# Two pages a step: sample attention over the paged cache in 16 steps

## The reference

```python
ckv_past = cache_ckv[page_table].reshape(b, past, KV_RANK)      # 8 x 2048 x 256
kr_past = cache_krope[page_table].reshape(b, past, QK_ROPE)     # 8 x 2048 x 64
keys_c = jnp.concatenate([ckv_past, ckv], axis=1)
keys_r = jnp.concatenate([kr_past, k_rope], axis=1)
sc = (einsum('bqhr,bkr->bhqk', q_lat, keys_c) + einsum('bqhe,bke->bhqk', q_rope, keys_r)) * SCALE
p = softmax(sc)
o_lat = einsum('bhqk,bkr->bqhr', p, keys_c)
```

## Time and profile before

| | |
|---|---|
| median of 3 runs | 669.1 us (668.73 to 670.76) |
| span of the profiled execution | 667.8 us, granted clock 0.927 |
| PE busy | 560.4 us, 84% |
| DVE, ACT, POOL busy | 359.6, 263.1, 162.3 us |
| DMA | 95.75 MB, mean 143 GB/s |

### The profile page before, as it was taken

The page is one execution under the profiler, slowest core; times in us unless marked ns, Lnnn a source line. Parts: engine busy times, 40 slices in busy tenths (PEclk is TensorE's granted clock), DMA queues, the critical chain, the costliest instruction groups (busy, mean ns, idle before and its releaser), DMA issues.

```text
span 667.8 us, 12482 instructions
## 1 busy us (share of the span) xinstructions
PE 560.4 (84%) x4724; PEld 469.1 (70%) x4724; DVE 359.6 (54%) x774; ACT 263.1 (39%) x571; POOL 162.3 (24%) x240
## 2 busy tenths in 40 slices
PE   2899998999999999999966146699885879999990
PEld 2799998999888888888743134345553548999980
DVE  4643987725666666444366266427775672323227
ACT  6413221123555554525143244337665552222210
POOL 4202000000000000000035274307998850112114
PEclk9989998969999999999997578799999799999996
DMA  7042122365888888887244632401232252332203
GB/s 294 32 158 95 49 90 71 113 227 164 261 270 267 267 265 272 276 272 238 87 117 100 186 100 75 182 1 44 83 101 89 95 219 99 97 92 82 80 1 128
DMA packets 46926, 95.75 MB, mean 143 GB/s; under 512 B 6489, under 2 KB 18114, under 8 KB 46354
## 3 DMA queue, kind: packets, MB, share of 16 engines
q1 hardware_dynamic: 46866, 94.94, 44.3%
HBM read 87.29 MB, written 7.73 MB: 142 GB/s over the span
## 4 chain that ended last, share of the span: by engine, by line
PE 60%; DVE 10%; POOL 8%; DMA 7%; issue 5%; ACT 4%; SPq 4%; DVEq 0%; POOLq 0%; ACTq 0%; PEldq 0%
PE pm L1163 16%; PE pm L1164 14%; PE pm L1165 14%; DMA dec<-ac_dram 4%; PE px L1225 4%; POOL xb L1137 3%; POOL hring L1142 3%; PE px L1241 3%; SPq L372 2%; PE pm L1400 2%; DVE xw_lo L787 1%; DVE r_pre L715 1%; POOL dec L1106 1%; PE pm L1447 1%; DMA w_raw<-in_w_out 1%
## 5 line engine op out<-in xcount | busy, mean ns | idle before, releaser
L1163 PE MATMUL pm<-xw_hi,w_lo 128*128 128x260 f32 x544 | 166.1, 305 | 15.9 <-DVE w_lo L685 11.4
L1164 PE MATMUL pm<-xw_lo,w_hi 128*128 128x260 f32 x544 | 157.1, 289 | 0.0
L1165 PE MATMUL pm<-xw_hi,w_hi 128*128 128x260 f32 x544 | 156.8, 288 | 0.0
L1163 PEld LDWEIGHTS pm<-xw_hi,w_lo 128*128 128x128 f32 x544 | 105.6, 194 | 33.0 <-issue 11.9
L425 ACT ACTIVATE w_hi<-w_raw 128x1024 fp32r<-128x1024 f32 (+1 forms) x56 | 57.8, 1032 | 154.5 <-PE pm L1165 153.9
L685 DVE TENSOR_TENSOR w_lo<-w_raw,w_hi 128x1024 fp32r<-128x1024 f32 (+1 forms) x56 | 67.9, 1214 | 80.6 <-ACT w_hi L425 80.5
L1164 PEld LDWEIGHTS pm<-xw_lo,w_hi 128*128 128x128 f32 x544 | 105.9, 195 | 0.2
L1165 PEld LDWEIGHTS pm<-xw_hi,w_hi 128*128 128x128 f32 x544 | 105.9, 195 | 0.0
L1163 PE MATMUL pm<-mix_hi,w_lo 128*128 128x260 f32 x256 | 72.4, 283 | 1.3 <-DVE mix_lo L986 1.3
L1164 PE MATMUL pm<-mix_lo,w_hi 128*128 128x260 f32 x256 | 72.5, 283 | 0.0
L1165 PE MATMUL pm<-mix_hi,w_hi 128*128 128x260 f32 x256 | 72.4, 283 | 0.0
(11 more groups left out here) (240 smaller groups left out, 1088.1 us busy)
## 6 DMA issues: line engine op xcount, KB each, us to landing
page<-in_cache SPq DMA_DIRECT2D x128, 288.0 KB, 3.4
w_raw<-in_w_in SPq DMA_DIRECT2D x34, 512.0 KB, 5.0
w_raw<-in_w_out SPq DMA_DIRECT2D x16, 512.0 KB, 3.6
dec<-ac_dram SPq DMA_DIRECT2D x16, 256.0 KB, 10.2
hring<-in_ssm_state SPq DMA_DIRECT2D x8, 512.0 KB, 3.5
o_ssms<-hring SPq DMA_DIRECT2D x8, 512.0 KB, 2.6
w_raw<-in_w_qb SPq DMA_DIRECT2D x6, 384.0 KB, 3.0
xraw<-in_xT SPq DMA_DIRECT2D x4, 520.0 KB, 6.0
```

Source lines behind the costliest of these rows:

```text
L1163: pe.matmul(out, wl, xh, start=start, stop=False)
L1164: pe.matmul(out, wh, xl, start=False, stop=False)
L1165: return pe.matmul(out, wh, xh, start=False, stop=stop)
```

## The change

A step is now two pages of four sequences: 16 steps, every 20 slots. Each has three places of its own: scores (`SLOT`), transposes (`TSLOT`, 10 slots on) and values (`VSLOT`, 16 slots on); all lie inside items 19 to 38. Keys and values are separate arrays in DRAM and separate buffers (`kpage`, `vpage`), each two steps deep, of the same total size. SyncE issues one DMA per sequence, page and kind: 8 of 160 KB for the keys of a step, 8 of 128 KB for its values. Steps 0 and 1 are loaded in rounds 15 and 16 of its loop; later, keys n+2 are loaded in the round after the item of scores n, and values n+2 in the round after the item of values n. The matmuls of the scores take the columns of both pages at once; values of the two pages are summed in PSUM. Probabilities and their transpose have one buffer in place of two.

```diff
-NSTEP = 2 * NPAGE
-SLOT = [divmod(16 * 19 + 3 + 32 * n // 3, 16) for n in range(NSTEP)]
-VSLOT = [divmod(min(16 * 19 + 32 * (n + 1) // 3 + 10, 16 * NIN - 1), 16) for n in range(NSTEP - 1)]
+PPS = 2
+SPG = NPAGE // PPS
+NSTEP = 2 * SPG
+SLOT = [divmod(16 * 19 + 3 + 20 * n, 16) for n in range(NSTEP)]
+TSLOT = [divmod(16 * 19 + 3 + 20 * n + 10, 16) for n in range(NSTEP)]
+VSLOT = [divmod(16 * 19 + 3 + 20 * n + 16, 16) for n in range(NSTEP)]
...
-    page = at("page", [P, 4, 4, 576], F, G_)
+    kpage = at("kpage", [P, 2, 4, PPS, 320], F, G_)
+    vpage = at("vpage", [P, 2, 4, PPS, 256], F, G_ + 20480)
...
-        def load_pages(n):
-
-            g, p, s = n // NPAGE, n % NPAGE, n % 4
-            if n >= 4:
-                sp.wait_ge(p_pn, n - 3)
+        def load_pages(what, n):
+
+            g, p0 = n // SPG, PPS * (n % SPG)
+            to, of, done, free = ((kpage, "cache_k", s_kl, p_sc), (vpage, "cache_v", s_vl, p_pn))[what]
+            if n >= 2:
+                sp.wait_ge(free, n - 1)
             for j in range(4):
-                at_ = (4 * g + j) * NPAGE + p
-                index = sp.value_load(ptab[0:1, at_:at_ + 1])
-                sp.dma_start(page[:, s, j, :], a["cache"][bass.ds(index, 1)].rearrange("a p n -> p (a n)")).then_inc(s_pl[s], 16)
+                for p in range(PPS):
+                    at_ = (4 * g + j) * NPAGE + p0 + p
+                    index = sp.value_load(ptab[0:1, at_:at_ + 1])
+                    sp.dma_start(to[:, n % 2, j, p, :], a[of][bass.ds(index, 1)].rearrange("a p n -> p (a n)")).then_inc(done[n % 2], 16)
...
-            for n in steps(i + 1):
-                load_pages(n)
+            if i in (15, 16, 17):
+                for what in range(2):
+                    if i < 17:
+                        load_pages(what, i - 15)
+            for n in steps(i - 1):
+                if n + 2 < NSTEP:
+                    load_pages(0, n + 2)
+            for n in sums(i - 1):
+                if n + 2 < NSTEP:
+                    load_pages(1, n + 2)
...
-            for n in steps(i):
-                if n:
-                    copy_ptb(n - 1)
-                sample_exp(n)
+            for place, do, n in sorted([(SLOT[n], 0, n) for n in range(NSTEP)] + [(TSLOT[n], 1, n) for n in range(NSTEP)]):
+                if place[0] == i:
+                    (sample_exp, copy_ptb)[do](n)
...
                     if 8 * r + k in place:
-                        n_ = place[8 * r + k]
-                        if n_:
-                            prob_t(n_ - 1)
-                        score(n_)
+                        score(place[8 * r + k])
+                    if (i, 8 * r + k) in TSLOT:
+                        prob_t(TSLOT.index((i, 8 * r + k)))
...
-            pe.wait_ge(s_pl[s], 64 * (n // 4 + 1))
+            pe.wait_ge(s_kl[n % 2], 64 * PPS * (n // 2 + 1))
+            out = px[:, n % 2, 0:PPS * P].rearrange("p (a k) -> p a k", a=PPS)
             for op in range(4):
                 for j in range(4):
...
-                    x = page[:, s, j, (256, 384, 512, 512)[op]:(384, 512, 576, 576)[op]]
-                    lo_, n_ = (0, 0, 0, 64)[op], (128, 128, 64, 64)[op]
-                    last = pe.matmul(px[32 * j:32 * j + 32, n % 2, lo_:lo_ + n_], w, x, start=op == 0, stop=op == 3)
+                    x = kpage[:, n % 2, j, :, (0, 128, 256, 256)[op]:(128, 256, 320, 320)[op]]
+                    half = slice((0, 0, 0, 64)[op], (128, 128, 64, 128)[op])
+                    last = pe.matmul(out[js, :, half], w, x, start=op == 0, stop=op == 3)
...
         def values(n):
             pe.wait_ge(a_ptb, n + 1)
+            pe.wait_ge(s_vl[n % 2], 64 * PPS * (n // 2 + 1))
             if n:
                 pe.wait_ge(v_upd, n)
-            for j in range(4):
-                last = pe.matmul(px[32 * j:32 * j + 32, 3, 0:KVR], ptb[:, n % 2, 32 * j:32 * j + 32], page[:, n % 4, j, 0:KVR],
-                                 start=True, stop=True)
+            for p in range(PPS):
+                for j in range(4):
+                    last = pe.matmul(px[32 * j:32 * j + 32, 3, 0:KVR], ptb[:, P * p + 32 * j:P * p + 32 * j + 32],
+                                     vpage[:, n % 2, j, p, :], start=p == 0, stop=p == PPS - 1)
...
-        prob_t(NSTEP - 1)
-        values(NSTEP - 1)
         o_lat_t(1)
```

More of the change, by code:

```diff
@@ L162, in build @@
     sqs = at("sqs", [P, TT], F, H_ + 5 * TB)
-    psm = at("psm", [P, 2, P], F, H_ + 3 * TB)
-    ptb = at("ptb", [P, 2, P], F, H_ + 4 * TB)
+    psm = at("psm", [P, PPS * P], F, H_ + 3 * TB)
+    ptb = at("ptb", [P, PPS * P], F, H_ + 4 * TB)
     o_lat = at("o_lat", [P, KVR], F, H_ + 5 * TB)
@@ L170, in build @@
                         ("xlast", [P, XT, 11]), ("dtt", [P, 80]), ("nacum", [P, 64]), ("toend", [P, 64]),
-                        ("ealast", [P, 64]), ("nmh", [P, 2, NPAGE + 1]), ("alpha", [P, NSTEP]), ("rs", [P, NSTEP]), ("lsum", [P, 2]), ("epsc", [P, 1]), ("nmx", [P, 8]),
+                        ("ealast", [P, 64]), ("nmh", [P, 2, SPG + 1]), ("alpha", [P, NSTEP]), ("rs", [P, NSTEP]), ("lsum", [P, 2]), ("epsc", [P, 1]), ("nmx", [P, 8]),
                         ("rsum", [P, 8])):
@@ L212, in build @@
     s_pt = sem("page_table_loaded")
-    s_pl = [sem(f"page_loaded{s}") for s in range(4)]
+    s_kl, s_vl = [[sem(f"page_{w}_loaded{s}") for s in range(2)] for w in ("keys", "values")]
     s_out = sem("stored")
@@ L258, in steps, with sums @@
         return [n for n, (item, k) in enumerate(SLOT) if item == i and r in (None, k // 8)]
-    def sums(i, r):
-        return [n for n, (item, k) in enumerate(VSLOT) if item == i and k // 8 == r]
+    def sums(i, r=None):
+        return [n for n, (item, k) in enumerate(VSLOT) if item == i and r in (None, k // 8)]
     def quarters_of(h):
@@ L473, in copy_ptb @@
             act.wait_ge(p_tr, n + 1)
-            if n >= 2:
-                act.wait_ge(p_pn, n - 1)
-            act.activation(ptb[:, n % 2, :], px[:, 2, 0:P], ACT.Copy).then_inc(a_ptb, 1)
+            if n:
+                act.wait_ge(p_pn, n)
+            act.activation(ptb, px[:, 2, 0:PPS * P], ACT.Copy).then_inc(a_ptb, 1)
         def sample_exp(n):
-            g, p = n // NPAGE, n % NPAGE
+            g, p = n // SPG, n % SPG
             act.wait_ge(v_smx, n + 1)
@@ L483, in sample_exp @@
                .then_inc(a_prob, 1)
-            if n >= 2:
-                act.wait_ge(p_tr, n - 1)
-            act.activation(psm[:, n % 2, :], px[:, n % 2, 0:P], ACT.Exp, bias=nmh[:, g, p + 1:p + 2],
+            if n:
+                act.wait_ge(p_tr, n)
+            act.activation(psm, px[:, n % 2, 0:PPS * P], ACT.Exp, bias=nmh[:, g, p + 1:p + 2],
                            accum_out=rs[:, n:n + 1]).then_inc(a_prob, 1)
@@ L544, in _ @@
                     silu_z(t)
-        copy_ptb(NSTEP - 1)
         for k in range(2):
@@ L694, in evac @@
                     do(n)
-                    if do is sample_sum and n == NPAGE:
+                    if do is sample_sum and n == SPG:
                         sample_out_t(0)
@@ L754, in sample_max @@
         def sample_max(n):
-            g, p = n // NPAGE, n % NPAGE
+            g, p = n // SPG, n % SPG
             dve.wait_ge(p_sc, n + 1)
-            link(dve.tensor_reduce(nmx[:, 0:1], px[:, n % 2, 0:P], AX.X, ALU.max, negate=True))
+            link(dve.tensor_reduce(nmx[:, 0:1], px[:, n % 2, 0:PPS * P], AX.X, ALU.max, negate=True))
             if p:
@@ L763, in sample_sum @@
         def sample_sum(n):
-            g = n // NPAGE
+            g = n // SPG
             own = lsum[:, g:g + 1]
@@ L773, in sample_sum @@
                .then_inc(v_upd, 1)
-            if n % NPAGE == NPAGE - 1:
+            if n % SPG == SPG - 1:
                 link(dve.reciprocal(nmx[:, 3:4], own))
@@ L880, in _ @@
                     conv(t)
-        sample_sum(NSTEP - 1)
         sample_out_t(1)
@@ L1211, in score @@
         def score(n):
-            g, s = n // NPAGE, n % 4
+            g = n // SPG
             if n == 0:
@@ L1231, in prob_t @@
                 pe.wait_ge(a_ptb, n)
-            if n == NPAGE + 1:
+            if n == SPG + 1:
                 pe.wait_ge(v_ol, 2)
-            pe.transpose(px[:, 2, 0:P], psm[:, n % 2, :], cm[:, M_ID, :]).then_inc(p_tr, 1)
+            for p in range(PPS):
+                last = pe.transpose(px[:, 2, P * p:P * p + P], psm[:, P * p:P * p + P], cm[:, M_ID, :])
+            last.then_inc(p_tr, 1)
         def values(n):
             pe.wait_ge(a_ptb, n + 1)
+            pe.wait_ge(s_vl[n % 2], 64 * PPS * (n // 2 + 1))
             if n:
                 pe.wait_ge(v_upd, n)
-            for j in range(4):
-                last = pe.matmul(px[32 * j:32 * j + 32, 3, 0:KVR], ptb[:, n % 2, 32 * j:32 * j + 32], page[:, n % 4, j, 0:KVR],
-                                 start=True, stop=True)
+            for p in range(PPS):
+                for j in range(4):
```

(7 more changed lines are left out.)

4 lines of the change are left out of this document (2 added, 2 removed).

## The result

The changed kernel takes 710.1 us (median; 707.8 to 712.5), the kernel before 668.9 us in the same comparison: a ratio of 1.065, with a 95% interval from 1.060 to 1.069. That is 41 us slower, where 26.5 us were forecast and 704 us was the upper end of the range. The direction and the place are as forecast, the size is not.

What follows compares the result with a forecast made beforehand. TensorE's stream bounds the stage before; SyncE's 256 page issues at 0.81 us bound it after. Stage end 24.8 us later plus 1.7 for the clock is 26.5; 669.1 + 26.5 = 695.6 us, range 688 to 704.

Steps and rivals of the forecast that it cites:

- What bounds: Stage from item 19 to o_lat's transpose: TensorE's stream bounds before; after, SyncE's issues, 13.6 us a pair step against 10.45.
- The pace of issues: SyncE's queue in the stage: 0.81 us per page issue with its number load, 208 issues taking 168.5 us.
- Early loads: SyncE's rounds 15 and 16: 32 issues, 25.9 us, fit before item 19; priced nothing, at most 2 us if late.
- the fourth part of the change: Loading steps 0 and 1 in SyncE's rounds 15 and 16, before item 19: priced nothing, at most 2 us.
- The landing behind the last issue: End of SyncE's page loads for values 14: the last DMA lands 2.7 us after its start, at 342.7 us.
- The two-page insertions: TensorE in the stage: scores of two pages 1.72 us in place of 2.12, values 1.20 in place of 1.54.
- TensorE's gain: TensorE in the stage: 0.49 us won per pair step, 7.8 us in all, if it were fed.
- rival A: SyncE's pace 0.64 us or less, TensorE stays the bound: stage ends at 324.2, -11.1 us, 658.0 us; chance 0.05.
- Part (5) of the change: DVE and ACT: half as many small sample instructions at twice the width; priced nothing while not behind TensorE.
- B: SyncE's loop: a pace in between, 0.65 to 0.70 us, giving about 662 to 673 us; chance 0.03.
- C: TensorE's clock falls in each step and stays low, last run of 17.4 us at half speed: 711 us; chance 0.05.
- D: SyncE's page number loads are slower, 492 ns each: pace 1.03 us, 741 us; chance 0.01.

Runs made afterwards that it cites:

- the fixed number: Changed kernel with a fixed page number in each page DMA in place of the number loaded from the table: 660.6 us, ratio 0.984.
- the split of the old kernel: Kernel before with each page DMA split into keys and values, each with its own page number load: 703.1 us, ratio 1.048.
- its shared load: Kernel before with each page DMA split into keys and values, one page number load for the two: 677.6 us, ratio 1.013.
- the last version: Against the kernel before: whole pages in one DMA, two-page steps, early loads in rounds 11 and 13: ratio 0.982; 652.5 to 659.9 us in four runs, 662.8 and 664.8 in two.

## Why the prediction was right in kind and short by 14 us

*What bounds.* Right. SyncE was off the path and is on it now. The test that carries this is the fixed number (0.46 us an issue, no gaps) together with the split of the old kernel (1.048) and its shared load (1.013). Theories of the transfers, the short rows and the insertions are out.

*The pace of issues: the term that was mis-sized.* From 171.47 to 355.53 us are 184.1 us for 208 page issues and 15 weights; I had 168.5 + 7.1 = 175.6, so 8.5 us were missing. 26 blocks of eight at an undisturbed 6.00 us would be 156; added up they are 7.2 us more, from some ten single issues of 0.7 to 1.8 us, and one weight DMA took 1.49 us in place of 0.42. That is 0.035 us an issue: the pace was 0.81 with nothing in the way and 0.84 to 0.85 on average. The trace of before had half of it. "max" is 877 beside a median of 333, and beside the 2.75 us of the block that I read there are blocks of four like this one:

```profile
289.44 3.21 SPq L302 DMA_DIRECT2D page<-in_cache  x4
```

From issue to issue inside the blocks of four, 96 times, the mean is 0.83 us; over 208 issues the 0.02 more make 4.4 of the missing 8.5 us. In the kernel after, long ones are more frequent (16 of 224 by over 0.3 us, against 5 of 96). I read the pace off two clean blocks and took the best case for the mean. While SyncE had spare time these long issues cost nothing, so nothing pointed at them. What makes an issue long stays open: they come at irregular distances, also with fixed numbers.

*Early loads: priced at nothing, cost about 5 us.* The other step that failed is the fourth part of the change. I checked item 19's weights against the time TensorE needs them, found that it fits, and priced the copies behind the split at 2 us at most. For item 18 I gave only the time its weights leave. What stood behind its split on VectorE, the rotations of q, I didn't ask. That path starts at the DMA, passes three queues and ends in a wait and a slower clock. Item 19 started 6.3 us late; 1.1 of these are the difference of the two profiled runs. With 16 early issues in the same two rounds instead of 32, TensorE starts item 19 at 151.1 us (whole pages, early loads in rounds 15 and 16); and spread over four rounds the 32 leave it 1.7 us late, 0.6 of them from before the loads.

*The rest of the sum held.* TensorE's waits for page DMAs are 30.7 us, within the 25 to 35 named beforehand. SyncE started 0.4 us later than worked out, after the shift. The landing behind the last issue took 0.3 us less. Behind values 14 TensorE took 18.6 us, against 17.4 plus 1.7 for the clock: 376.14 less 357.50, and the first matmuls behind the gap are slow (1.72 us for the values in place of 1.07, with a granted clock of 0.63 from 357 to 360 us). Together: 360.1 + 1.7 + 6.3 + 0.4 + 8.5 - 0.3 - 0.5 = 376.2, and the trace has 376.14. The stretch behind was 2.6 us shorter in the profiled run; its granted clock is 0.88 in both, so what made it shorter isn't shown. The two-page insertions cost what was worked out: scores 318.95 - 317.30 - 0.12 + 0.11 = 1.64 us (1.72), values 1.20 (1.20). TensorE's gain is real and was hidden; it appears in the last version, whose stage ends at 325.6 where 324.2 was worked out for rival A. It starts there at 150.3 us, so it is 175.2 us long against the 173.0 worked out. Part (5) of the change had nothing for waits for ScalarE, and TensorE has 3.9 us of them there, 6.9 in the changed kernel.

*The rivals.* A, a pace below 0.64, fell: none was seen with number loads. Of B the idea was right (each 0.01 us is 2 us) but on the other side: the doubt was about a pace read too slow, and the measured mean was slower still. C fell: the clock did drop behind gaps (0.94 from 290 to 320 us), but it is 1.00 again from 363 us to the end of the stage, and the last run of TensorE was 1.2 us longer than worked out at full clock. That it comes back so soon isn't in the earlier trace rows, which end at 0.67; the trace of before has 1.00 from 107 to 110 us. D fell: the loads take 269 ns again. The floor of about 600 ns that the Trainium skill gives for such a load (DMA: Bandwidth & Descriptors, "Latency and other measured facts") doesn't show here: the load adds 0.35 us to the pace, 0.81 less 0.46. The range was too narrow because its spread for the pace, 0.80 to 0.83, came from the same two blocks, and it had 2 us for everything that could happen before the stage.

## What to carry to other kernels

Count instructions of the issuing queue as work of an engine: number of issues times pace, against the period of the stage, before anything is said of bytes. Splitting a DMA whose address is loaded costs the load twice; share the load or don't split. Take the pace as a mean over the stage with its long ones, not from a clean block. And for DMAs that are moved ahead of others in a queue, follow each thing that is now later through every queue it passes, not only to its first reader.

## What the runs showed of the hardware that I had not expected

One issue from SyncE takes 0.46 us with a fixed address and 0.81 us with a page number loaded from SBUF, though the load itself shows as 0.27 us; two issues on one load take 1.33 us. One issue in 14 took 0.3 to 1.5 us longer in the changed kernel (16 of 224), one in 20 with a fixed number (11 of 224, by up to 1.0 us), one in 19 in the kernel before (5 of 96, by up to 0.5 us). Rows of 1280 and 1024 bytes instead of 2304 cost little: 293 GB/s at a share of 0.92, against 291 GB/s at 0.89 with whole rows (the fixed-number and the last kernel). And the clock granted in the sparse stage behind differs from run to run: 0.72 and 0.80 over 110 us in two profiled runs with the same program there, which are 10 us apart in it.
